# A two-layer attention trunk on one core: value products ahead of the transposes and the scores in every even step

## The reference, cut to what matters

```
layer 0:  h = rmsnorm(x); q, k, v = h @ w_in            # 16 heads of 64
          mixer A, 8 heads: softmax(q k' / 8 + bias over dilated windows) v
          mixer B, 8 heads: the same on a 64-wide grid, 8 rows x 16 columns of neighbours
          x += concat(heads) @ w_out;  x += swiglu(rmsnorm(x))
layer 1:  low-rank q and kv, 64 + 32 dimensions a head, 16 heads, dense
          o = softmax((q k' + rotary part) * scale + bias) v
          x += o @ w_out;  x += swiglu(rmsnorm(x));  out = rmsnorm(x)
```

## Time and profile before

| | |
|---|---|
| median of 3 runs | 2824.0 us (2819.72 to 2824.43) |
| the profiled execution | 2822.84 us, its span 2821.0 us |
| mean granted TensorE clock | 0.987 |
| TensorE matmuls | 2703.4 us busy, 96% of the span |
| VectorE, ACT, POOL | 61%, 34%, 51% |
| attention of layer 0 | about 78 to 655 us |
| attention of layer 1 | about 1502 to 2026 us |

### The profile page before, as it was taken

The page is one execution under the profiler, slowest core; times in us unless marked ns, Lnnn a source line. Parts: engine busy times, 40 slices in busy tenths (PEclk is TensorE's granted clock), DMA queues, the critical chain, the costliest instruction groups (busy, mean ns, idle before and its releaser), DMA issues. The chain is left out here.

```text
span 2821.0 us, 41222 instructions
## 1 busy us (share of the span) xinstructions
PE 2703.4 (96%) x13508; PEld 2242.6 (79%) x13508; DVE 1734.4 (61%) x2819; ACT 954.2 (34%) x1774; POOL 1435.4 (51%) x1348
## 2 busy tenths in 40 slices
PE   6899999989999999999998999999999999999996
PEld 3788888877877888788767888888887878878875
DVE  6466666664755555555576777777567555555555
ACT  3455555562411100001135666666533000111002
POOL 2333344356756555556643333343765556665554
PEclk9999999999999999999999999999999999999998
DMA  4433334444311211111234433334432111112112
GB/s 137 128 88 79 93 77 101 95 140 129 99 45 45 59 52 45 52 56 48 60 105 115 110 95 88 102 88 127 142 101 64 45 52 57 47 52 60 45 45 75
DMA packets 273162, 228.59 MB, mean 81 GB/s; under 512 B 44537, under 2 KB 237425, under 8 KB 272849
## 3 DMA queue, kind: packets, MB, share of 16 engines
q1 hardware_dynamic: 271223, 222.33, 28.4%
q10 hardware_dynamic: 1811, 4.64, 0.4%
HBM read 158.22 MB, written 17.04 MB: 62 GB/s over the span
## 5 line engine op out<-in xcount | busy, mean ns | idle before, releaser
L763 POOL TENSOR_SCALAR xT<-xT,rden 128x1024 f32<-128x1024 f32 (+2 forms) x256 | 280.8, 1097 | 651.9 <-DVE rden L1892 651.9
L804 POOL TENSOR_TENSOR ring<-block_t,ring 128x512 fp32r<-128x512 f32 x312 | 410.5, 1316 | 24.9
L1900 DVE TENSOR_TENSOR pt<-psD,pt 128x512 fp32r<-128x512 f32 (+2 forms) x512 | 303.3, 634 | 133.4 <-ACT pt L1458 132.9
L1142 PE MATMUL psS<-times_r,ring 128*128 128x512 f32 x928 | 366.8, 395 | 16.5 <-ACT rstd L1567 9.4
L802 POOL CAST ring<-block_t 128x512 fp32r<-128x512 f32 x312 | 209.3, 671 | 321.8 <-PE psD L1176 138.3
L1144 PE MATMUL psS<-times_r,ring 128*128 128x512 f32 x928 | 362.9, 391 | 0.0
L1143 PE MATMUL psS<-times_r,ring 128*128 128x512 f32 x928 | 362.9, 391 | 0.0
L2064 DVE TENSOR_TENSOR xT<-psD,xT 128x512 f32<-128x512 f32 x320 | 218.7, 690 | 176.1 <-PE psD L1176 176.1
L1458 ACT ACTIVATE pt<-psD 128x512 fp32r<-128x512 f32 (+2 forms) x512 | 257.8, 557 | 151.2 <-PE psD L977 150.4
L1884 DVE CUSTOM_DVE_ANT_0 xT<-psS,xT 128x1024 f32<-128x1024 f32 (+2 forms) x256 | 287.3, 1122 | 1.8 <-PE psS L964 0.9
L1447 ACT ACTIVATE xT<-xT,mneg 128x1024 f32<-128x1024 f32 (+2 forms) x256 | 273.6, 1069 | 31.4 <-DVE mneg L1884 31.4
(11 more groups left out here) (293 smaller groups left out, 4987.4 us busy)
## 6 DMA issues: line engine op xcount, KB each, us to landing
block_t<-in_w_gate SPq DMA_DIRECT2D x96, 256.0 KB, 2.9
block_t<-in_w_up SPq DMA_DIRECT2D x96, 256.0 KB, 3.2
block_t<-in_w_down SPq DMA_DIRECT2D x88, 256.0 KB, 3.1
kq<-split_x SPq DMA_DIRECT2D x130, 128.0 KB, 2.4
kq<-row SPq DMA_DIRECT2D x126, 128.0 KB, 2.3
xT<-rel_c SPq DMA_DIRECT2D x16, 960.0 KB, 5.4
stage<-in_w_even SPq DMA_DIRECT2D x24, 512.0 KB, 3.7
heads<-o_out SPq DMA_DIRECT2D x128, 64.0 KB, 2.1
```

The lines of the kernel that those rows point to most:

```text
L763: pool.tensor_scalar(s, s, rden[:, t % 4:t % 4 + 1], 1.0, ALU.mult, ALU.mult).then_inc(S["normed"], 1)
L804: pool.tensor_tensor(lo, src, hi.bitcast(F32), ALU.subtract).then_inc(S["ws"], 1)
L1142: pe.matmul(o, unit(u, 0)[:, w], hi, start=first and k == 0, stop=False)
L1900: ve.tensor_tensor(PT[:, 1, j0:j1, t % 3, :], blocks(psT[b][:, 0:(j1 - j0) * P]), PT[:, 0, j0:j1, t % 3, :].bitcast(F32), ALU.subtract).th ...
```

## The change

In both attention loops of TensorE the call of `values` in even steps moves from behind `scores` to the head of the step. Nothing else is touched, on TensorE or on another engine.

```diff
@@ layer 0
             for t in range(-1, TILES + 3):
                 pair, step = t // NSTEP, t % NSTEP
+                if t >= 4 and t % 2 == 0:
+                    values(0, (t - 4) // 2, window_even)
                 if 2 <= t < TILES + 2:
                     turn_scores(0, t - 2, window_even)
                 if t + 1 < TILES:
...
                     scores(0, t + 1, window_even, even_operands)
-                if t >= 4 and t % 2 == 0:
-                    values(0, (t - 4) // 2, window_even)
                 if step in (2, 3) and 0 <= pair < PAIRS:
                     turn_v(0, pair, step - 2)
@@ layer 1
+                if t >= 4 and t % 2 == 0:
+                    values(TILES, (t - 4) // 2, window_c)
                 if 2 <= t < TILES + 2:
                     turn_scores(TILES, t - 2, window_c)
...
                     for n in (3, 5):
                         c_product(0, n)
-                if t >= 4 and t % 2 == 0:
-                    values(TILES, (t - 4) // 2, window_c)
```

## The result

| | before | after |
|---|---|---|
| median | 2823.8 us (2819.7 to 2824.4) | 2938.2 us (2937.4 to 2941.3, 4 runs) |
| ratio of the runs side by side | | 1.041 (1.0395 to 1.0426) |
| span of the profiled execution | 2821.0 | 2936.3 |
| mean granted TensorE clock | 0.987 | 0.980 |

The changed kernel is 4.1% slower. The direction was forecast, the size was not: 115 us of span against 76, and 2938 lies above the stated 2925.

What follows compares the result with a forecast made beforehand. TensorE was taken to bound attention, except for short waits. Added waits of 18.8 + 35.7 + 17.4 + 4 = 75.9 us on 2822.84 gave 2898, range 2853 to 2925, chance 0.62.

Steps and rivals of the forecast that it cites:

- The odd T's wait: Layer 0: odd-step score transposes wait for PSUM banks, 0.49 us in mixer A, 0.6 in mixer B; sum 18.8.
- V's wait behind the chain of `sum_o`: Steps without long products: value products wait for a chain 6.0 us after the even transposes; 1.5 in layer 1.
- V's wait in step 4: Step 4: with the values' transposes in the chain, value products wait about 1.9 us in layer 1; layer 0 adds 0.5.
- rival D: Clock falls to 1.2 GHz for some 3 us at 15 head-pair changes: 45 us more, 2943; chance 0.08 shared with upper bound.
- With 2.04 it is 6.55, nothing: Layer 1, steps after nine-matmul products: 2.04 us of product makes TensorE's time 6.55 against 6.0, so value products wait nothing.
- three and three: Layer 0's changes of head pair: net 3.4 us three times in mixer A, 2.4 three times in mixer B; sum 17.4.
- layer 0's start and last head pair: At both ends of layer 0, value-product waits partly replace waits for POOL's scores: between 0 and 9 us, taken as 4.
- mixer A's head pairs: Mixer A's head pairs would take 5.8 us more; growth over 8 or under 3 would show the forecast wrong.
- The clock sign: A granted clock below 0.97 in the attention windows would show the forecast wrong.
- A: Value products wait only from their own tile's transposes, without exp and bias ahead: 38 us more, 2861; chance 0.20.
- B: Faster: value products fill the transposes' wait for banks, 23 us go: 2800 with no odd wait; chance 0.05.
- C: No change that can be told, within 0.2% (5.6 us): waits only move from transposes to value products; chance 0.05.

Runs made afterwards that it cites:

- e5: Changed kernel, with VectorE doing bias_scores of odd steps after keep_p_lo and sum_o instead of before: 2962.3 us, ratio 1.0489.
- e3: Changed kernel, with ten useless matmuls run ahead of the value products in step 4 of each head pair: 2923.0 us, ratio 1.0352.
- e10: Changed kernel, with the value products back behind scores in steps 6, 8 and 10 of layer 1: 2928.7 us, ratio 1.0371.
- e8: Changed kernel, with the value products back behind scores in step 10 of layer 1 only: 2939.2 us, ratio 1.041.
- e12: Kernel before, from each layer's second head pair: scores, transposes, value products in step 2, and, except in last pairs, in step 4 with early value eviction: 2816.2 us.
- e6: Changed kernel, with ACT and VectorE taking out the second half of the values in step 3 instead of step 4: 2923.7 us, ratio 1.0361.

## Why the prediction was wrong, by its own steps

**The odd T's wait: right.** Per two steps, 0.49 was forecast in mixer A, and it is 0.48 to 0.51 in all 20 intervals from steps 6 to 14; 0.6 in mixer B, where it is 0.39 to 0.81 with a mean of 0.64; nothing in layer 1, where steps 6 are within 0.04. In sum 19.6 against 18.8.

**V's wait behind the chain of `sum_o`: right where that chain ends last.** Step 0: 1.93 forecast in mixer A (6.0 - 4.07) and 2.00 measured; 1.5 in layer 1 and 1.52 measured; steps 12 and 14 of layer 1 0.8 each, and 0.77 and 0.84 measured. V is covered by the long products, as said. That `bias_scores` belongs to the chain is borne out by the second wait line of e5.

**V's wait in step 4: the step that failed.** The forecast said "with turn_v in between (its eviction and keep_v_lo lie in the same chain) about 1.9", and for layer 0 "turn_v behind a later keep_v_lo 0.5". The chain was taken to end with `sum_o`, 6.0 us after the even T, with 0.4 to 0.5 more for turn_v. On the timeline above it is 184.87 - 176.85 = 8.0. One part is the first half of the values, whose eviction (0.59) and low part (0.69) stand ahead of the bias: it starts at 180.88 and not at 176.85 + 0.70 + 0.95 + 1.40 = 179.9. The other is the second half, which the forecast never named as an operand of V, and which comes 1.1 us after V would have had the rest. The code has this wait right behind the two lines that were quoted as the wait of V that matters:

```
if g % 8 == 0:                    # the first call of a head pair
    pe.wait_ge(S["v_lo"], (t0 + 2 * g) // 8 + 2)
```

In layer 1 V's idle time in step 4 is 2.56 us where 1.9 was forecast (1.66 in the first head pair), in mixer A 3.13 where it was 1.93 + 0.5, in mixer B 2.65 where it was 1.3 + 1.0; idle times come out short, so the gap is wider. Before, T and S lay ahead of V and hid it: the trace before showed this wait 4 times with 2.1 us in all, so only the code could have told what it would become. Steps 0 to 4 grew by 11.7 us more than forecast without the clock, 3.5 in mixer A, 2.3 in mixer B and 5.9 in layer 1. Most of that is this wait; some is waits before T that were counted as gone and were smaller.

**The clock: rival D, taken as unlikely and needed as a part.** D set 45 us, for 15 changes of head pair (there are 14) at 3 us, with 0.08. It happened as a mechanism: e3 measures 15 us. It was too dear by three: ten of the 14 changes are hit, and one costs 1.1 to 2.3 us, not 3. Its chance was too low, because it was weighed against waits of 1.0, and not against the 1.9 to 2.4 that the forecast itself put in step 4. And the trace before had a row between the two that wasn't read. In the earlier trace rows the last head pair of layer 0 stands at 0.97 and was taken as a sign against D; within it the clock fell once, behind a wait of 2.23 us. Both rows are of the kernel before:

```profile
637.26 0.80 PE L1062 MATMUL psD<-hT,W 128*128 128x512 f32 x1 [2.23 <-POOL hT L769]
```

```profile
637.00:640.40 3.40, 3.14 (x10) 2.68 (x11) 0.23 (x1) 0.66 (x2) 3.40 (x3) 0.51 0.00 0
```

D's chance should have been weighed against that. The Trainium skill, "TensorE: Matmul & The Clock Gate", section "HAM oscillation", says that gaps between matmul groups bring the half clock back; the trace agrees, with 0.72 in the window behind a wait of 3.13.

**Step 10 of layer 1: not seen, 8.6 us.** The forecast said "With 2.04 it is 6.55, nothing". For V that is right. It costed V's own wait and the odd T's, and did not follow what a later even T does to ACT, to the evictions and to SP's transfers, though T, on which they hang, is what the move pushes back. e10 shows that it goes with V's place in steps 6, 8 and 10; e8 shows that step 10 alone isn't the cause.

**One change of head pair was not counted.** Layer 0 has seven: three in mixer A, three in mixer B and the one between them. The forecast priced three and three. The one between measures 1.78 + 1.97 + 0.50 = 4.2 us, 1.1 of it the clock.

The account of the 39 us, from the intervals of both traces: the clock behind V of step 4 14.1, by e3's trace; steps 0 to 4 without it 11.7; step 10 8.6; the change left out 3.2 without its clock; the last head pair of layer 1 1.8 without its clock. The odd T's 0.8 more and the 0.8 less of layer 0's start and last head pair cancel.

**Its own signs.** Of what it named as a sign of being wrong, one came: mixer A's head pairs grew by 8.2 to 9.1 us, over the 8. The clock sign, 0.97 in the attention windows, didn't come in windows of a head pair (0.98 to 1.00 where there are products); the fall showed in windows of 4 to 6 us (0.57 and 0.72).

**The rivals.** A (38 us, V waits for its own tile alone) is refuted by every step 0 and by e5. B, that V fills the wait of T, has nothing for it: V waited in the steps without a product around every change of head pair. Of its thought the opposite is true: S can fill it (e12). C is out.

**Left open.** With the same wait of 2.56 us before V of step 4, the clock fell in four of seven head pairs of layer 1 and stayed in three; with 2.65 in mixer B it fell in three of four. No run tells these apart.

## What to carry to other kernels

When an instruction is moved to the head of an in-order queue, list every semaphore it waits on from the code, those of its first call in a group too. The waits that show in the trace before are only those that were not hidden, and the move takes the cover from all of them. Then follow the instructions that were pushed *back* by the move: T came 1.9 us later in steps in which V cost nothing, and the bill came in step 10 by way of ACT and a DMA queue. In a group of three pieces, try first the one that needs least that is fresh: of the three orders tried around a change of head pair, S, T, V was the fastest (by 0.13 to 0.25% against T, S, V) and V, T, S the slowest. And look at the clock in windows as short as the wait: over a head pair a fall hides in the second decimal.

## What the runs showed of the hardware

A single short wait of TensorE, busy before and behind it, can cost it the clock. In the changed kernel the granted clock fell to its lower level, 1.2 GHz, behind V's wait in step 4 in 10 of 16 places: behind 3.13 us in three of three, behind 2.65 in three of four, behind 2.56 in four of seven, but not behind 2.96 and 1.66 in the first head pairs. It also fell at waits of 1.81 in two places (T at 1969.93, and V in step 8 of layer 0's last head pair). After the wait of 3.13 it was back after V's 16 and T's 8 matmuls (S at 189.21 took 1.17 us). Behind the wait of 1.70 at 174.87 it stayed at 2.4 GHz. With waits of 2.9 to 4.6 us in these places (e5) it fell in all 16, with 1.5 to 2.6 us (e6) in 8, and with the waits filled (e3) in none. So length alone doesn't decide it. Ten matmuls without use in such a wait were worth 15 us over 16 waits; where it can't be removed, filling it is a gain.
